# Closing and opening matrix stages with weights as the moving operand, in two passes over token halves

## The reference, cut to what matters

```python
u = rmsnorm(h, g_pre)
z = u @ w_in
...                                   # attention, gated recurrences
y = concat(...) @ w_out               # 2048 -> 2048
h = h + rmsnorm(y, g_post)
# layer 0 only:
gate = sigmoid(h @ w_pg)              # 2048 -> 2048
e = p @ w_pp
h = h + rmsnorm(gate * e, g_ple)
```

## Time and profile before

| | before |
|---|---|
| median of 3 runs | 3030.28 us (3029.82 to 3030.91) |
| span of the profiled execution | 3028.2 us |
| PE busy | 2952.6 us (98%) |
| DVE / ACT / POOL busy | 1652.3 / 1284.4 / 1313.5 us |
| HBM traffic | 285.67 MB read, 100 GB/s over the span |

### The profile page before, as it was taken

How to read it: one execution, slowest core, us unless ns; L and a number is a source line. 1 busy time by engine, 2 the same in 40 slices (tenths; PEclk the granted TensorE clock), 3 DMA queues, 4 the chain that set the end, 5 groups by cost and what they waited for, 6 DMA issues and landing times.

```text
span 3028.2 us, 48369 instructions
## 1 busy us (share of the span) xinstructions
PE 2952.6 (98%) x17162; PEld 2383.7 (79%) x17162; DVE 1652.3 (55%) x2349; ACT 1284.4 (42%) x2468; POOL 1313.5 (43%) x1002
## 2 busy tenths in 40 slices
PE   8999999999999999989999999999999999999997
PEld 6888888877777787767887878788778878787886
DVE  5367666655657315657565664551275666654412
ACT  6445444354547333444333333453343333344432
POOL 4444444433343343553444444444544444434444
PEclk9999999999999999999999999999999999999999
DMA  6223222222222324234222222242242222222322
GB/s 239 101 91 111 83 82 72 82 84 83 71 81 84 126 97 139 98 111 142 87 87 91 89 96 74 80 153 97 97 156 94 95 88 89 84 84 83 140 97 97
DMA packets 60880, 305.72 MB, mean 101 GB/s; under 512 B 5712, under 2 KB 6096, under 8 KB 29776
## 3 DMA queue, kind: packets, MB, share of 16 engines
q1 hardware_dynamic: 38224, 259.54, 23.9%
q10 hardware_dynamic: 22528, 44.50, 4.3%
HBM read 285.67 MB, written 18.35 MB: 100 GB/s over the span
## 4 chain that ended last, share of the span: by engine, by line
issue 56%; POOL 32%; PE 9%; POOLq 1%; DMA 1%; ACT 1%; DVE 1%; DVEq 0%; ACTq 0%; SPq 0%
POOL w_low L262 31%; PE z L325 8%; DMA w_raw<-in_wt 1%; POOLq L261 1%; POOL next_weights L270 0%; PE scores L325 0%; PE v_bank L358 0%; PE z L358 0%; ACT u_high L722 0%; DVE mixed L1649 0%; POOLq L296 0%; DVE work L1268 0%; POOLq L284 0%; POOLq L129 0%; ACT w_high L710 0%
## 5 line engine op out<-in xcount | busy, mean ns | idle before, releaser
L262 POOL TENSOR_TENSOR w_low<-w_raw,w_high 128x512 fp32r<-128x512 f32 x932 | 1252.7, 1349 | 1695.1 <-ACT w_high L710 1687.5
L325 PE MATMUL z<-u_high,w_high 128*128 128x512 f32 x3408 | 1347.5, 395 | 2.5 <-POOL w_low L262 1.8
L325 PE MATMUL z<-u_high,w_low 128*128 128x512 f32 x3408 | 1328.5, 390 | 0.0
L325 PE MATMUL z<-u_low,w_high 128*128 128x512 f32 x3408 | 1327.0, 389 | 0.0
L710 ACT ACTIVATE w_high<-w_raw 128x512 fp32r<-128x512 f32 x928 | 578.7, 628 | 1219.4 <-PE z L325 1128.7
L325 PEld LDWEIGHTS z<-u_high,w_high 128*128 128x128 f32 x3408 | 640.1, 188 | 159.6 <-issue 23.3
L325 PEld LDWEIGHTS z<-u_high,w_low 128*128 128x128 f32 x3408 | 639.7, 188 | 136.0
L325 PEld LDWEIGHTS z<-u_low,w_high 128*128 128x128 f32 x3408 | 640.5, 188 | 127.7
L1635 DVE TENSOR_TENSOR work<-work 128x512 f32<-128x512 f32 x87 | 99.7, 1146 | 365.2 <-ACT work L949 351.9
L1262 DVE TENSOR_TENSOR work<-z,work 128x512 f32<-128x512 f32 x110 | 76.1, 691 | 123.7 <-PE z L325 103.0
L1294 DVE SCALAR_TENSOR_TENSOR work<-z,work 32x512 f32<-32x512 f32 (+1 forms) x176 | 120.9, 687 | 2.4
(11 more groups left out here) (281 smaller groups left out, 3234.4 us busy)
## 6 DMA issues: line engine op xcount, KB each, us to landing
w_raw<-in_wt SPq DMA_DIRECT2D x241, 1024.0 KB, 4.8
out_hT<-work ACTq DMA_DIRECT2D x8, 1024.0 KB, 8.7
work<-out_hT ACTq DMA_DIRECT2D x8, 1024.0 KB, 10.3
work<-in_xT SPq DMA_DIRECT2D x4, 1024.0 KB, 17.0
e_scratch<-work ACTq DMA_DIRECT2D x1, 4096.0 KB, 16.5
work<-in_xT ACTq DMA_DIRECT2D x4, 1024.0 KB, 11.1
work<-in_dec ACTq DMA_DIRECT2D x12, 256.0 KB, 2.7
work<-rope_tables ACTq DMA_DIRECT2D x10, 256.0 KB, 2.8
```

The lines of the kernel that those rows point to most:

```text
L262: pool.tensor_tensor(WL[:, 4 * q:4 * q + 4, :], RAW[:, t.odd, 512 * q:512 * q + 512].rearrange("p (k c) -> p k c", k=4), WH[:, 4 * q:4 * q ...
L325: mm = pe.matmul(bank[:], w[:, k, :], u[:, k, :], start=(k == 0 and n == 0), stop=(k == KT - 1 and n == 2))
```

## The change

The last four tiles of each closing stage (`w_out` of all layers, `w_pg`) and the first four of each stage behind one (`w_pg`; in layers 1 and 2 the four `dv` tiles, moved there from the steps of the attention) no longer run tile by tile. Four tiles together run in two **passes**, one for each half of the 512 tokens. In a pass (`one_pass`) blocks of 128 tokens of `u` are stationary and 512 weight columns move: 16 steps of 6 matmuls, so 96 matmuls of 512 columns for four tiles and half the tokens. The result has tokens on partitions. Both passes need all weights of the four tiles, so these are loaded and split twice: the list has 270 tiles in place of 242, and tiles of passes are loaded in four parts of 256 KB.

Since a token is now a partition, the sum of its last 512 squares comes from ACT's accumulator (`block_square`), and the factor of a half (`token_root`) is turned into a row by a matmul of ones with a diagonal matrix (`root_row`). The last four tiles of `y`, scaled, are turned back by PE transposes (`turn_back`). While half 1 is in its pass, half 0 is normalized, added to `h` and split (`residual_half`, `high_half`, `low_half`); half 1 follows in the next stage's first pass, which works on half 0. The gate stage also turns back its first four tiles. The three-quarter steps of the attention spread 12 quarters over the 16 points of a step.

```diff
+            def one_pass(t, h, g=None, order=range(KT), behind=5, between={}, updated=None):
+                pe.wait_ge(sem("z_free"), t.times(1, 1 - T_HGG - behind))
+                if updated is not None:
+                    pe.wait_ge(sem("h_new"), updated)
+                for n, k in enumerate(order):
...
+                    pe.wait_ge(sem("h_ready"), tt.times(4, q + 1))
+                    if g is not None:
+                        pe.wait_ge(sem("u_half"), (2 * g + h) * KT + n + 1)
+                    for x in range(2):
+                        pe.matmul(PASS_BANK[h][x][:], UH[:, k, tokens[x]], high, start=(n == 0), stop=False)
+                        pe.matmul(PASS_BANK[h][x][:], UL[:, k, tokens[x]], high, start=False, stop=False)
+                    pe.wait_ge(sem("l_ready"), tt.times(4, q + 1))
+                    for x in range(2):
+                        mm = pe.matmul(PASS_BANK[h][x][:], UH[:, k, tokens[x]], low, start=False, stop=(n == KT - 1))
+                    mm.then_inc(sem("w_free"), 1)
+                    if n in between:
+                        between[n]()
...
+            def norm_points(n, h, pg=False):
+                if pg:
+                    return {13: lambda: root_row(n),
+                            15: lambda: turn_back((sem("y_scaled"), 4 * h + 4), h, (0, 12), BACK_PG[h])}
...
+                return {3: lambda: root_row(n),
+                        4: lambda: turn_back((sem("z_free"), t - T_HGG - PASS + PASS * h), h, (12,), BACK)}
-            sum_rows_last(16)
-            three_tiles(Tile(T_PG), 2)
...
+            close_first(T_OUT + OUT_CLOSE, SQ_OUT + OUT_FULL)
+            one_pass(Tile(T_OUT + OUT_CLOSE + PASS), 1, between=norm_points(0, 0))
+            one_pass(Tile(T_PG), 0, 0, ORDERS[0], between=norm_points(1, 1))
+            one_pass(Tile(T_PG + PASS), 1, 0, ORDERS[0])
...
+            close_first(T_PG + PG_CLOSE, SQ_PG + PG_FULL)
+            one_pass(Tile(T_PG + PG_CLOSE + PASS), 1, between=norm_points(2, 0, True))
...
+                one_pass(Tile(base), 0, l + 1, ORDERS[l + 1], updated=2 * KT + 12 if first else None,
+                         between=norm_points(2 * l + 3, 1, first))
+                one_pass(Tile(base + PASS), 1, l + 1, ORDERS[l + 1], updated=3 * KT + 12 if first else None)
```

On ACT, work is laid between the splits of a pass (`passing`: after split n the entries of the list under n):

```diff
+            def norm_work(t, n, h, g):
+                at = {0: [lambda: pass_squares(t, h), lambda: token_root(n, h)],
+                      1: [lambda: scaled_block(h, 0), lambda: scaled_block(h, 1)]}
+                if g == 0:
+                    for p, m in ((9, 0), (11, 4), (13, 8), (15, 12)):
+                        at[p] = [lambda m=m: high_half(0, h, m, 4)]
+                elif g is not None:
+                    for p in range(8, 16):
+                        at[p] = [lambda m=m: high_half(g, h, m) for m in (2 * p - 16, 2 * p - 15)]
...
+            def gate_norm_work(h):
+                rows = [2 * h, 2 * h + 1, 2 * h + 12, 2 * h + 13]
+                return {0: [lambda: gate_exp(rows[2])], 1: [lambda: gate_exp(rows[3])], 5: [lambda: gate_square(rows[2])],
+                        9: [lambda: gate_square(rows[3]), lambda: token_root(2 + h, h)],
+                        **{10 + i: [lambda r=r: gate_scaled(h, r)] for i, r in enumerate(rows)},
+                        15: [lambda n=n: high_half(1, h, n) for n in range(KT)]}
...
+                squares_at = {n: [lambda n=n: square(n)] for n in range(KT)}
+                squares_at[0] = [store_h] + squares_at[0]
+                passing(Tile(base + PASS), squares_at)
```

More of the change, by code:

```diff
@@ L877, in _, with step @@
             WORK = {"hg": hg_work, "att": att_work, "ret": ret_work, "dif": dif_work}
[L879 removed]
+            def step(t, gate=None, gates=None, hg=None, work=None, j=None, apart=False, between={}, behind={}, quarters=QUARTERS, **kw):
                 for p in range(16):
[L882 removed]
+                    s, q = quarters.get(p, (None, None))
                     if t is not None and apart and s == 3:
                         for n in range(4 if q == 0 else 0):
[L885 to L886 removed]
+                            high_apart(t.plus(4), n)
+                    elif t is not None and p in quarters:
                         high(t.plus(s), q)
@@ new lines, in passing, with block_square, pass_squares @@
+            def passing(t, work={}, last=False):
+                for n in range(3 * PASS if last else 4 * PASS):
+                    high(t.plus(n // 4), n % 4)
+                    for w in work.get(n, ()):
+                        w()
+            def block_square(src, h, x, col):
+                act.activation(row(SQ0 + x), src, ACT.Square, accum_out=tk(col + 2 * h + x)).then_inc(sem("block_squared"), 1)
+                act.drain()
+            def pass_squares(t, h):
+                act.wait_ge(sem("w_free"), t.times(4, 4 * PASS))
+                for x in range(2):
+                    block_square(PASS_BANK[h][x][:], h, x, TS)
@@ L937, in squares, with out_slots, one @@
                         high(t, m // 4)
-            def out_slots(t, n, gain, root, loads=(), last="next", pair=False):
-                def one(tt, m, s, used, first=False, quarters=4, taken=None, bank=None):
-                    for q in range(quarters):
-                        if not first:
-                            high(tt, q)
+            def out_slots(t, n, gain, block, loads):
+                def one(tt, m, s, used, bank, weights=True, taken=None):
+                    for q in range(4 if weights else 0):
+                        high(tt, q)
                     act.wait_ge(sem("w_free"), tt.times(4, 4) if taken is None else taken)
                     act.wait_ge(sem("sq_used"), PRIMED + used)
-                    bank = Z[s] if bank is None else bank
                     act.activation(row(SQ0 + s), bank[:], ACT.Square).then_inc(sem("sq_ready"), 1)
@@ L1678, in layer_params, with low_halves @@
+            def low_halves(g, h):
+                for n in range(0, KT, 4 if g == 0 else 1):
+                    low_half(g, h, n, 4 if g == 0 else 1)
             def layer_params(l):
```

726 lines of the change are left out of this document (395 added, 331 removed).

## The result

The changed kernel takes **3083.5 us** (median of 4 runs, 3082.5 to 3086.5); the kernel before, run beside it, 3030.6 us (3029.8 to 3032.8). The ratio is 1.0175, 95% interval 1.0162 to 1.0187: 53 us slower, where 3026.4 was forecast and 3044 was the upper bound. The profiled execution has a span of 3081.6 us.

What follows compares the result with a forecast made beforehand. The prediction took PE, busy 98%, as the bound, so time falls only where PE stands still or its work shrinks. 56.0 us given back less 52.1 taken left 3.9 net: 3026.4 us, range 3004 to 3044.

Steps and rivals of the forecast that it cites:

- The attention steps: Attention with three tiles per step: softmax has little time left to PE's turn; 0.5 us per step, 4 us (0 to 12).
- Rival D: Attention steps: work between quarters, not the tiles, sets their pace; 2 us in each of 8 steps, 3038 us; chance 0.08.
- The second passes: Second passes of layers 1 and 2: ACT's issuing (4.9 us) and DVE's sums delay weight splits; 6.0 us each, 12 together.
- Loading is no term: Weight loading in passes costs nothing: 4 MB in 21.7 us is 193 GB/s, and 363 were moved at layer 1's start.
- Out-projection to gates: First seam: the factor causes no wait; POOL, held up by DVE, is 0.7 us late per half, 1.4 us.
- Gates to layer 1: Gate seam: PE waits for DVE's low parts behind both halves, plus lower clock and 3 us for `gate_square`; 15.8 us.
- Layer 1 to layer 2: Seam between layers: second half's token sums stand behind DVE's low parts, so PE waits for the row; 2.4 us.
- PE's own additions: Extra PE work at the passes: transposes and rows 7.5 us, gate stage's transposes 5.1, one-column sums 2.6; together 15.2 us.
- the end: Kernel's end: only half the tokens left to normalize, add and store; 17.5 us instead of 20.7, so 3.2 saved.
- the start: Kernel's start: PE's first step needs two quarters instead of one; 1.3 us more.
- Rival B: Passes: stalls hide, DVE and POOL fit each other's gaps, tables don't block ACT; 3008 us (3000 to 3018), chance 0.32.
- Rival C: All passes: POOL, slowed by the lock with DVE, sets the pace, over 95% busy; 28 us more, 3054 us; chance 0.15.

Runs made afterwards that it cites:

- No-LRU: Changed kernel with DVE's LRU work for the last retention head left out of each layer's first three-tile step (one row tile wrong): 3068.1 us against 3083.5.
- Fourth quarters: Changed kernel with each three-tile-step point that had no quarter repeating the previous one, 87.0 us of added matmuls without new weights: 3145.4 us against 3083.5.
- both gate-order runs: DVE makes four low parts before the remaining residual rows: 3090.6 us against changed 3083.5; with ACT's high parts split, on the kernel with spread stores (3076.7): 3080.0.
- three edits: Changed kernel with loads of e spread, second-pass squares through PSUM and stores of h spread, all together: 3070.1 us against 3083.5.
- three reorderings: Changed kernel (3083.5 us) with, singly, DVE's gate-seam residual order changed (3090.6), head copies ahead of the LRU chain (3091.8), LRU gate work earlier (3092.0).

## Why the prediction was wrong

Of the 57 us between 3026.4 and 3083.5 the attention steps carry 26, the seam from layer 1 to layer 2 12, that from the out-projection to the gates 10, and that from the gates to layer 1 5. The other 4 are small: 2.5 are the half clock in the gate tiles behind the first seam (granted clock 0.58 from 1216 to 1222 us).

**The attention steps: forecast 4 (bounds 0 to 12), measured about 30.** This is the step that failed. In layer 1 PE's four steps took 50.2, 49.5, 51.7 and 51.6 us before and 41.7, 47.8, 41.6 and 41.7 after. A removed tile is worth 10.9 and a turn 0.5, so the steps lose 2.4, 9.7, 1.4 and 1.3 us, about 15 in all, and as much in layer 2. The prediction put 0.5 us on each, because "three tiles leave 40.2" of 51.6 us while DVE is busy 25.2 in the earlier trace rows; it named this term as one "read from no row". That row is a step in the middle of the differential attention. At the head of the second step PE waits for the last retention head's LRU gates, a chain of some 17 us on DVE that already ended with PE waiting for it before. I took one step's row for all eight. No-LRU (15.4 us less, the second step 8.9 shorter in each layer) shows that this chain is the cause of about half. Fourth quarters shows that the removed tile had been the cover of nearly all of it: 25.1 of 87.0 us of PE work cost nothing. The rest, 1.3 to 2.4 us in each of the other steps, I only read from the waits: 2.0 us for ACT in the first step, up to 0.8 for the turns L643. Rival D had the right mechanism at 2 us in each of 8 steps; it is one step of nearly 10 us and three of 1 to 2 in each layer.

**The second passes: forecast 6.0 over each, measured 10.3 and 12.4.** Mechanism right, size off: the term "4.9 us" for ACT's issuing took 0.46 for a table from the earlier trace rows, where the table is issued 22 us after the stores. Right behind them the three tables took 4.45, 1.46 and 1.25 us in layer 2, and the seven instructions held ACT 11.2 us (7.7 in layer 1). "Loading is no term" failed with it: it compared 193 with 363 GB/s and left out the 4.75 MB that come beside them. Together 8.75 MB in a pass of 21.7 us would be 403 GB/s. Spreading them brought 6.8 us. The contention of DVE and POOL, the other half of this term, was right: 1.65 forecast and 1.70 measured per step with a sum of squares, and removing it brought 5.3 us.

**Out-projection to gates: forecast about 5 us over, measured 15.** Part is the same omission: 4 MB of `e` loaded in a pass of layer 0, a 4.3 us wait behind the last pass, and half clock behind that; spreading brought 4.0 us by the median. In the passes themselves PE waits seven times up to 0.6 us, 3.5 in all, for POOL and once for DVE, while DVE makes residual additions and `u_low` of 1024 elements (1.90 us each); the forecast of 0.7 us late per half was too small. It was not tested by itself.

**Gates to layer 1: forecast 27 over, measured 33.** The two pauses behind the turned rows came, at 6.1 and 6.8 us (4.4 forecast), with 1.2 GHz for about a dozen matmuls behind each (granted clock of 0.91 over the stretch). The 3 us for `gate_square` did not come. The cause of the pauses was read rightly as DVE's chain; but both gate-order runs show that a shorter first wait alone gives nothing: the low parts then run beside POOL, the gate product comes later, and the wait that the prediction had for `gate_square` appears, at 9 to 10 us.

**Layer 1 to layer 2: forecast 12 over, measured 24.** `token_scale` behind the low parts came as said, but as a wait of 4.9 us instead of 2.4, since the low parts run 1.44 us apart beside POOL (about 0.40 without), and with a stretch of half clock behind it (0.66 from 2220 to 2230 us) that the forecast left out. The remainder is the second pass above.

**PE's own additions** were mis-sized in one place: the one-column sums, 2.6 us in the forecast (24 times its 0.13 is 3.1). Each shows as two records 0.11 us apart, so 24 take 5.4.

**Right:** the end (tail 5.4 us shorter where 3.2 was forecast, passes 2.3 longer where about 2 was, so 3.1 in all instead of 1), the start (1.6 us more wait, 1.3 forecast), and the places of the waits at the seams. Rival B (the stalls hide) is disproved by all of it. Rival C had POOL as the pace of all passes, with POOL over 95% busy; it was busy 91, 78 and 83% over the three seams, and it was the pace only where DVE had two-operand sums. The range was too narrow because bounds of 0 to 12 for the steps came from a row that didn't cover the worst of them.

What stays open: which order at the gate seam frees both queues, the part of the attention's 30 us beyond the LRU chain, and the rest of the first seam and of layer 2's first pass, which were only read from the waits. No run undoes all of it: what the experiments took away, 13.4 us with three edits and 15.4 without the LRU chain, is half of the 57.

## What to carry to other kernels

A tile that is moved out of a step takes its cover along. Before counting it as a gain, look at the step with the longest chain on another engine, not at a typical one, and compare that chain with what PE has left. A wait of 0.17 us in the list of before is the sign that such a chain has no room. When passes read weights twice as fast, every other transfer that falls into them has to be counted in MB and spread; a burst holds the engine that issues it. And a wait that is removed shows its worth only if nothing stands behind it in the same in-order queue: three reorderings here lost 7 to 9 us each.

## What of the hardware was unexpected

- Issuing is not a fixed cost. One 1 MB store took 0.39 us to issue alone and a 256 KB table 4.45 us when four stores had been issued just before.
- A short DVE instruction with one operand in SBUF can be held up too. The one on the diagonal (128x128, `token_scale`) takes 0.29 us while POOL is idle; the two that began between POOL's splits at the first seam took 1.13 and 1.32:

```profile
1166.15 2.38 DVE L1806 TENSOR_SCALAR token_scale<-identity,token_norm 128x128 f32<-128x128 f32 x2 [0.63 <-ACT token_norm L1023]
```

- DVE's low parts of 256 elements start 0.40 us apart while POOL is idle and 1.44 apart beside it.
- The changed family scatters more, 0.7 to 8.9 us between the runs of one kernel against up to 3.2 for the one before; why was not looked into. Differences below 3 us were told from traces only, or not at all.
